# A hybrid decoder layer on one core: four edits in the order of ScalarE, in the head norms and in the branch stage

## The chip, the core and the metric

The kernel runs on one core of one Trainium2 chip. The metric is the device time of one execution in microseconds, the median of several. Engines: TensorE (PE, weight loads PEld), VectorE (DVE), ScalarE (ACT), GpSimd (POOL), SyncE (SP, which issues nearly all DMAs).

## The reference

One layer of a decoder on 1024 prompt tokens and 32 sample tokens (8 sequences of 4), model width 1024, all fp32. After an RMS norm one projection gives everything: queries, keys and values of branch A, the q/k/v channels and the gates of branch B, queries of branch C, and 3 x 1024 gate columns.

- Branch A: attention in a sliding window of 128 with a sink, 8 heads of 64 on 2 key heads.
- Branch B: a causal convolution of width 4 over 1536 channels, Silu, and the gated delta rule on 4 heads of 128. Its q and k are normalised per head and token: `x * rsqrt(sum(x * x) + eps)`. Eight such sums per token (4 heads of q, 4 of k) are the head squares.
- Branch C: attention to 256 memory rows, 4 heads of 128.

```python
up = jnp.einsum('blnc,ncd->blnd', branches, p['w_branch'])
gate = jax.nn.sigmoid(gates.reshape(Bsz, L, N_BRANCH, D_MODEL))
mix = jnp.sum(gate * up, axis=2) @ p['w_out']
x = x + _rms_norm(mix, p['ln_mix_post'])
h = _rms_norm(x, p['ln_ffn_pre'])
gt, uf = jnp.split(h @ p['w_ffn_in'], 2, axis=-1)
f = (jax.nn.silu(gt) * uf) @ p['w_ffn_out']
x = x + _rms_norm(f, p['ln_ffn_post'])
```

## The kernel before, in words

The 1056 token columns lie along the free axis in 3 chunks of 352. A weight panel is 128 output channels by 1024 inputs. Each fp32 product is made from three fp32r products: weights and activations are split into a high part (rounded) and a low part (what remains), and high x high, high x low and low x high are summed. GpSimd splits each panel in two passes (L853 high, L856 low; in the branch stage L922 and L924, in `split_to`) from `raw` into `wsp`, both with two slots: one panel is used while the next is split and the one after it is loaded. The semaphores `w_hi` and `w_lo` count these passes.

**First projection (to about 384 us).** 27 panels by `gemm` (L995, 72 matmuls). Panels 0 to 11 are branch B's channels: ScalarE evicts them into `cv`, VectorE runs the convolution, ScalarE the Silu into `y2`; for panels 0 to 7 ScalarE also writes the squares into `sqb`. `head_squares(n)` (L1000) runs on TensorE behind `gemm(n + 3)`: for each of the 9 token tiles the 128 tokens of `sqb` are the stationary operand and one column of ones the moving one, so that tile t's sum lands in a column of its own of bank 4, with the tokens along the partitions. That is how VectorE needs them in `ssq`, which ScalarE fills at L1733 behind the evictions of the narrow panel 12 (L1069, `b` and `a` of branch B). These gemms stand in a loop of four rounds of two panels.

**Tiles (385 to 863 us).** For each of 8 tiles of 128 tokens all engines follow one list, `TILE`. Each engine has its own reading of a step. "G" is a number of matmuls of the gate panels, laid between the others as cover. S(j) is a pair of score products of branch A (j below 4) or C: TensorE makes them, VectorE takes the row maximum (L2313, L2321), ScalarE exponentiates (L1846). T(j) transposes the result on TensorE, V(j) multiplies it with the values. Y(l) and X(l) are the two halves of level l of the inversion of branch B's triangular matrix: Y's product is copied to `yy` by ScalarE (L1833), and X (L1183, L1186) multiplies with `yy`. In ScalarE's reading the exponentials of S(j) belong to step S, so for j = 1 and j = 2 they stand ahead of the copies of Y(1) and Y(4).

**Samples (863 to 1014 us).** The same for the sample tokens, with eight more gate panels between. `gates(x)` evicts a gate chunk and stores it. ScalarE's last function other than a copy there is a square root (L1949).

**Branch stage (1014 to 1163 us).** 12 panels j of 256 output channels by 512 inputs (L1500), 4 per branch, each of two halves by three chunks in banks 0 to 2. ScalarE takes the Sigmoid of the two gate rows of the panel (L1967, loaded by `load_q`), VectorE multiplies the bank with them (L2548 for the first branch; L2553 into `prd` and L2555 into `accT` later) and so frees it. The three branches' activations come from memory into `brw` (`load_br`) and are split into `actD` by ScalarE and VectorE (L1957 and L2505 by chunk for the first, L1963 and L2523 later). Between the branch panels the eight parts of `w_out` are loaded and split: ScalarE makes the high part (L1979), GpSimd the low part (L943), in the order `W_SEQ`. SyncE issues in this order at the front: `load_wb(0)`, `load_br(0)`, `load_wb(1)`, gates 0 and 1, the store `o_z`, then it waits for `g_ad` and issues eight stores of the recurrent state (L750), the store `mem_o`, `load_br(1)`, and in the loop over j the next panel and the next gates.

Then follow the output projection (L1523), the norms and the FFN (L1508, L1569), which nothing of the change touches.

## Time and profile before

| | us |
|---|---|
| median of 3 executions | 2065.21 (2065.07 to 2067.7) |
| the profiled execution's own time | 2062.75 |
| its span in the profile | 2060.9 |

| engine | busy us | share |
|---|---|---|
| VectorE | 987.8 | 48% |
| ScalarE | 517.7 | 25% |
| GpSimd | 742.3 | 36% |

The mean granted clock is 0.997 of full speed. Most of TensorE's work is the fp32r matmul of 352 columns; a record of one lasts 323 ns, but they are pipelined and follow each other by about 160. In the rows below a line begins with start and length in us, and a bracket at its end is the idle time of the engine ahead of it and what ended that. PEld rows tell better than PE rows when TensorE could have gone on, since the ends of matmuls are modelled.

### The profile page before, as it was taken

What the parts mean: (1) busy time and instruction counts of PE and PEld (TensorE: products, weight loads), DVE (VectorE), ACT (ScalarE), POOL (GpSimd) and SP (SyncE); (2) the same over time, 40 slices, a digit from 0 to 9 for tenths busy, and PEclk for the clock granted to TensorE, in tenths of its full rate; (3) what the DMA queues carried; (4) which work ended last, traced back from release to release, by engine and by line L of the source; (5) the groups of instructions that cost most, each with busy time, mean ns of one, the idle gap of its engine ahead of it and who ended that gap; (6) DMA issues with size and microseconds to landing.
All of it is one profiled execution on the core that took longest, in us unless ns stands there. A gap on an engine that the chain in (4) does not pass through costs nothing.

```text
span 2060.9 us, 36132 instructions
## 1 busy us (share of the span) xinstructions
PE 2002.7 (97%) x14350; PEld 1903.8 (92%) x14350; DVE 987.8 (48%) x1761; ACT 517.7 (25%) x1151; POOL 742.3 (36%) x318
## 2 busy tenths in 40 slices
PE   6999999999999999999999999999999999999998
PEld 6999999888888889989799888999999999999997
DVE  6755630356565555322459745434353525253535
ACT  5333621243343444321232333100000000000002
POOL 3434774222111122123145322443434343434344
PEclk9999999999999999999999999999999999999999
DMA  5223333433233332263674421111111111111114
GB/s 189 92 83 100 109 114 99 146 105 88 61 99 88 100 91 68 78 190 120 204 247 159 150 104 67 42 51 41 51 41 51 41 51 41 51 41 51 41 41 179
DMA packets 221294, 193.91 MB, mean 94 GB/s; under 512 B 24731, under 2 KB 192283, under 8 KB 221170
## 3 DMA queue, kind: packets, MB, share of 16 engines
q1 hardware_dynamic: 207058, 182.72, 28.7%
q10 hardware_dynamic: 14128, 9.65, 1.6%
q8 instruction: 79, 1.29, 0.3%
q14 instruction: 29, 0.24, 0.0%
HBM read 146.26 MB, written 47.09 MB: 94 GB/s over the span
## 4 chain that ended last, share of the span: by engine, by line
PE 91%; DVE 3%; DMA 2%; ACT 1%; issue 1%; SPq 1%; POOL 0%; ACTq 0%; DVEq 0%; POOLq 0%
PE psum L1508 24%; PE psum L995 13%; PE psum L1569 11%; PE psum L1200 9%; PE psum L1523 5%; PE psum L1500 4%; PE psum L1278 4%; PE psum L1112 3%; PE psum L1247 2%; PE psum L1183 1%; PE psum L1236 1%; PE psum L1019 1%; PE psum L1060 1%; PE psum L1186 1%; ACT pr L1846 1%
## 5 line engine op out<-in xcount | busy, mean ns | idle before, releaser
L853 POOL TENSOR_TENSOR wsp<-raw,kc 128x1024 fp32r<-128x1024 f32 x115 | 279.5, 2430 | 1101.6 <-PE psum L1200 391.6
L1508 PE MATMUL psum<-actD,wsp 128*128 128x352 f32 x3168 | 515.8, 323 | 1.0 <-ACT sg L2052 0.6
L1508 PEld LDWEIGHTS psum<-actD,wsp 128*128 128x128 f32 x3168 | 509.0, 188 | 1.6 <-issue 0.9
L856 POOL TENSOR_TENSOR wsp<-raw,wsp 128x1024 fp32r<-128x1024 f32 x115 | 283.7, 2467 | 9.0
L995 PE MATMUL psum<-actT,wsp 128*128 128x352 f32 x1656 | 269.6, 323 | 0.0
L2640 DVE TENSOR_TENSOR accT<-accT,psum 128x352 f32<-128x352 f32 x504 | 241.7, 520 | 50.1 <-PE psum L1569 50.1
L995 PEld LDWEIGHTS psum<-actT,wsp 128*128 128x128 f32 x1656 | 264.8, 188 | 0.3
L1569 PE MATMUL psum<-fT,wsp 128*128 128x352 f32 x1512 | 249.8, 323 | 0.4 <-DVE accT L2640 0.4
L1569 PEld LDWEIGHTS psum<-fT,wsp 128*128 128x128 f32 x1512 | 244.0, 188 | 0.7 <-DVE accT L2640 0.7
L1200 PE MATMUL psum<-actT,wsp 128*128 128x352 f32 x1152 | 229.6, 338 | 0.0
L2623 DVE TENSOR_TENSOR fr<-psum,sg 128x352 f32<-128x352 f32 x66 | 34.5, 524 | 375.3 <-PE psum L1508 373.1
L1200 PEld LDWEIGHTS psum<-actT,wsp 128*128 128x128 f32 x1152 | 183.3, 189 | 4.1
L1500 PE MATMUL psum<-actD,wsp 128*128 128x352 f32 x864 | 142.1, 326 | 7.9 <-DVE prd L2553 3.8
L1500 PEld LDWEIGHTS psum<-actD,wsp 128*128 128x128 f32 x864 | 139.9, 190 | 10.1 <-DVE prd L2553 4.7
L2052 ACT ACTIVATE sg<-psum 128x352 f32<-128x352 f32 x66 | 30.5, 464 | 435.1 <-PE psum L1508 435.1
L1278 PE MATMUL psum<-actT,wsp 128*128 128x352 f32 x576 | 104.1, 331 | 0.0
L1278 PEld LDWEIGHTS psum<-actT,wsp 128*128 128x128 f32 x576 | 92.2, 190 | 5.5 <-issue 5.2
L2060 ACT ACTIVATE fT<-fr 128x352 fp32r<-128x352 f32 x66 | 32.8, 498 | 230.5 <-DVE fr L2623 230.5
L2137 DVE SCALAR_TENSOR_TENSOR y<-cv,scT,y 128x1024 f32<-128x1024 f32 x72 | 62.4, 913 | 0.9 <-DVE y L2137 0.4
L2134 DVE TENSOR_SCALAR y<-cv,scT 128x1024 f32<-128x1024 f32 (+1 forms) x24 | 29.8, 1283 | 59.1 <-ACT y L1700 55.4
L2222 DVE TENSOR_TENSOR kd<-psum,par 128x512 f32<-128x512 f32 x8 | 5.5, 692 | 105.5 <-PE psum L1121 105.5
L922 POOL TENSOR_TENSOR wsp<-raw,kc 128x1024 fp32r<-128x1024 f32 x13 | 25.8, 1981 | 77.7 <-DMA raw<-in_w_branch 40.6
(452 smaller groups left out, 2484.8 us busy)
## 6 DMA issues: line engine op xcount, KB each, us to landing
raw<-in_w_in SPq DMA_DIRECT2D x100, 256.0 KB, 4.0
raw<-in_w_ffn_in SPq DMA_DIRECT2D x88, 256.0 KB, 3.1
gat<-s_gate SPq DMA_DIRECT2D x12, 1056.0 KB, 5.0
raw<-in_w_ffn_out SPq DMA_DIRECT2D x44, 256.0 KB, 2.7
s_gate<-gst SPq DMA_DIRECT2D x48, 176.0 KB, 1.9
s_qkv<-y SPq DMA_DIRECT2D x12, 528.0 KB, 3.0
brw<-s_br SPq DMA_DIRECT2D x3, 2112.0 KB, 9.5
raw<-in_w_branch SPq DMA_DIRECT2D x24, 256.0 KB, 5.6
```

The lines of the kernel that those rows point to most:

```text
L853: pool.tensor_tensor(wsp[:, slot, 0], raw[:, slot], ones.unsqueeze(1).to_broadcast([P, KT, P]), ALU.mult).then_inc(w_hi, 1)
L856: pool.tensor_tensor(wsp[:, slot, 1], raw[:, slot], wsp[:, slot, 0].bitcast(F32), ALU.subtract).then_inc(w_lo, 1)
L995: mm = pe.matmul(psum[0:m, c, 0:CH], wsp[:, slot, a, k, 0:m], actT[:, h, k, CH * c:CH * c + CH], start=(k == 0 and q == 0), stop=(k == KT ...
L1112: mm = pe.matmul(psum[:, bank, w * h:w * h + w], lhs(h), rhs(h), start=True, stop=True)
L1200: mm = pe.matmul(psum[:, x % 2, 0:CH], wsp[:, (NPB + j) % 2, a, kt, :], actT[:, h, kt, CH * c:CH * c + CH], start=(n % 24 == 0), stop=(n % ...
L1278: mm = pe.matmul(psum[:, c, 0:CH], wsp[:, (NPB + m) % 2, a, k, :], actT[:, h, k, CH * c:CH * c + CH], start=(y % 24 == 0), stop=(y % 24 == ...
L1500: mm = pe.matmul(psum[:, c, 0:CH], slab(wsp[:, :, a], slot)[:, k, P * half:P * half + P], actD[:, h, a4 + k, CH * c:CH * c + CH], start=(k ...
L1508: mm = pe.matmul(psum[:, bank, 0:CH], wsp[:, slot, a, k, :], actD[:, h, k, CH * c:CH * c + CH], start=(k == 0 and q == 0), stop=(k == KT - ...
L1523: mm = pe.matmul(psum[0:rows, 3 + 2 * slot + half, :], actD[:, h, (k + 4) % 8, P * t:P * t + rows], wo_part(k, a)[:, 512 * half:512 * half ...
L1569: mm = pe.matmul(psum[:, 4 + x % 4, 0:CH], wsp[:, slot, a, m, :], fT[:, fs, h, CH * c:CH * c + CH], start=(q == 0), stop=(q == 2))
L2137: op = dve.scalar_tensor_tensor(out=dst[part], in0=src[part], scalar=w, in1=dst[part], op0=ALU.mult, op1=ALU.add)
L2640: dve.tensor_tensor(accT[:, m, cols], accT[:, m, cols], psum[:, 4 + x % 4, 0:CH], ALU.add).then_inc(o_ad, 1)
```

## The change

1. **Head squares.** The squares are now the moving operand and a 32-column stationary operand `row_n` is zero but for column n, which is one. The 1024 prompt tokens go as four groups of 256 columns into four groups of 32 partitions of bank 4, the 32 sample tokens into bank 3. All eight heads accumulate in the same place (`start` at n = 0, `stop` at n = 7). The loop of panels is unrolled, since n sets `start` and `stop`. The sums then have tokens along the free axis: ScalarE copies them to `mout`, TensorE transposes them with three instructions behind the narrow panel, and ScalarE copies into `ssq` after the Silu of panel 11. `one_col` lies in `tmp`, written by three small memsets at GpSimd's start.
2. **TILE.** A new step Z(j), read by ScalarE only, holds the exponentials of S(j). Z(1) stands behind Y(1) and Z(2) behind Y(4), each other Z directly behind its S.
3. **Front of the branch stage.** Branch panel 2 is loaded ahead of SyncE's wait for `g_ad`. ScalarE runs a Sigmoid of one column ahead of the eviction of the last three gate chunks. The Sigmoid of gate panel 0 runs in two halves, and VectorE waits for the first only before it multiplies the first three chunks.
4. **Quarter passes.** In `split_to` and the low part of a `w_out` panel, a pass over 1024 columns becomes four over 256, with one semaphore increment behind the last.

```diff
+    one_col = tmp[:].rearrange("p x t h -> p (x t h)")[:, 0:40]
-    TILE = (... ("S", 1), ("Y", 1), ("G", 4), ... ("S", 2), ("Y", 4), ("G", 4), ...)
+    TILE = (... ("S", 1), ("Y", 1), ("Z", 1), ("G", 4), ... ("S", 2), ("Y", 4), ("Z", 2), ("G", 4), ...)
@@ sync
         store_dec(1, "o_z")
+        load_seq(2, 3)
         sp.wait_ge(g_ad, 8)
...
             if j + 2 < 12:
-                load_seq(W_N["b", j + 1] - NPD + 1, W_N["b", j + 2] - NPD + 1)
+                if j > 0:
+                    load_seq(W_N["b", j + 1] - NPD + 1, W_N["b", j + 2] - NPD + 1)
@@ gpsimd
+        pool.memset(one_col[:, 0:7], 0.0)
+        pool.memset(one_col[:, 7:8], 1.0)
+        pool.memset(one_col[:, 8:40], 0.0)
...
-            pool.tensor_tensor(hi, src, ones[:, 0:1].to_broadcast([P, D]), ALU.mult).then_inc(w_hi, 1)
+            for k in range(0, D, 256):
+                op = pool.tensor_tensor(hi[:, k:k + 256], src[:, k:k + 256], ones[:, 0:1].to_broadcast([P, 256]), ALU.mult)
+            op.then_inc(w_hi, 1)
             pool.wait_ge(w_hi, n + 1)
-            pool.tensor_tensor(lo, src, hi.bitcast(F32), ALU.subtract).then_inc(w_lo, 1)
+            low_part(n, hi, lo)
+
+        def low_part(n, hi, lo):
+
+            src = raw[:, n % 2].rearrange("p k n -> p (k n)")
+            for k in range(0, D, 256):
+                op = pool.tensor_tensor(lo[:, k:k + 256], src[:, k:k + 256], hi[:, k:k + 256].bitcast(F32), ALU.subtract)
+            op.then_inc(w_lo, 1)
@@ tensor
             pe.wait_ge(sq_ok, n + 1)
-            for t in range(NT + 1):
-                r = P if t < NT else NS
-                mm = pe.matmul(psum[0:r, 4, bass.ds(n * (NT + 1) + t, 1)], sqb[:, P * t:P * t + r], ones[:, 0:1],
-                               start=True, stop=True)
+            row_n = one_col[:, 7 - n:39 - n]
+            for g in range(4):
+                pe.matmul(psum[32 * g:32 * g + 32, 4, 0:2 * P], row_n, sqb[:, 2 * P * g:2 * P * g + 2 * P],
+                          start=(n == 0), stop=(n == 7))
+            mm = pe.matmul(psum[0:32, 3, 0:NS], row_n, sqb[:, SEQ:SEQ + NS], start=(n == 0), stop=(n == 7))
             mm.then_inc(ss_mm, 1)
...
-        with pe.Fori(0, 4) as i:
-            for b in range(2):
-                gemm(2 * i + 3 + b, 1 - b)
-                head_squares(2 * i + b)
+        for n in range(8):
+            gemm(n + 3, 1 - n % 2)
+            head_squares(n)
...
+        pe.wait_ge(sq_ok, 8 + 1)
+        for u in range(2):
+            pe.transpose(psum[:, 4, P * u:P * u + P], mout[:, 0, P * u:P * u + P], ident)
+        pe.transpose(psum[0:NS, 3, 0:32], mout[0:32, 0, 2 * P:2 * P + NS], ident[0:32, 0:32]).then_inc(ss_mm, 1)
@@ scalar
         act.wait_ge(ss_mm, 9)
+        act.activation(mout[:, 0, 0:2 * P], psum[:, 4, 0:2 * P], ACT.Copy)
+        act.activation(mout[0:32, 0, 2 * P:2 * P + NS], psum[0:32, 3, 0:NS], ACT.Copy).then_inc(sq_ok, 1)
...
-        ssps = psum[:, 4, 0:8 * (NT + 1)].rearrange("p (n t) -> p n t", n=8)
-        act.activation(ssq[:, :, 0:NT], ssps[:, :, 0:NT], ACT.Copy)
-        act.activation(ssq[0:NS, :, NT:NT + 1], ssps[0:NS, :, NT:NT + 1], ACT.Copy).then_inc(ssq_ok, 1)
         silu(11, 1, 16 * 5 + 16)
+        act.wait_ge(ss_mm, 10)
+        for u in range(2):
+            act.activation(ssq[:, :, u:NT:2], psum[:, 4, P * u:P * u + P].rearrange("p (g n) -> p n g", n=32)[:, 0:8, :], ACT.Copy)
+        act.activation(ssq[0:NS, :, NT], psum[0:NS, 3, 0:8], ACT.Copy).then_inc(ssq_ok, 1)
...
+                elif step[0] == "Z":
+                    j = step[1]
                     act.wait_ge(a_nm, 6 * t + j + 1)
...
         gates(20)
+        act.activation(dsm[:, 18:19], dsm[:, 1:2], ACT.Sigmoid)
...
             act.wait_ge(q_in[j % 2], 16 * (j // 2) + 16)
+            if j == 0:
+                act.activation(gat[:, 0, 0], gat[:, 0, 0], ACT.Sigmoid).then_inc(q_sg, 1)
+                act.activation(gat[:, 0, 1], gat[:, 0, 1], ACT.Sigmoid).then_inc(q_sg, 1)
+                return
@@ vector
-            dve.wait_ge(q_sg, j + 1)
+            dve.wait_ge(q_sg, j + 2 if j > 0 else 1)
...
             for half in range(2):
+                if j == 0 and half == 1:
+                    dve.wait_ge(q_sg, 2)
```

## Rows read from the trace of the kernel before

**Rows 1.** The page, part 1: busy us (share of span), instructions, per engine.
```profile
PE 2002.7 (97%) x14350; PEld 1903.8 (92%) x14350; DVE 987.8 (48%) x1761; ACT 517.7 (25%) x1151; POOL 742.3 (36%) x318
```

**Rows 2.** Waits of TensorE: engine, line, releaser: us in total, times, longest.
```profile
PE psum L1183 <- ACT yy L1833: 20.9, 16, 1.6
...
PE psum L1500 <- DVE prd L2553: 3.8, 3, 1.8
```

**Rows 3.** The chain in order of time: start us, us, what. Panels 3 and 11.
```profile
67.51 11.53 PE psum L995 x72
...
175.74 11.72 PE psum L995 x72
```

**Rows 4.** Timeline 900 to 910, TensorE, last row its weight loads.
```profile
900.72 1.09 PE L1337 MATMUL psum<-kc,ck 128*128 128x128 f32 x8
901.57 2.96 PE L1278 MATMUL psum<-actT,wsp 128*128 128x352 f32 x17
904.46 0.64 PE L1344 MATMUL psum<-ckT,qw 128*32 128x256 f32 x8
...
905.03 0.85 PEld L1337 LDWEIGHTS psum<-kc,ck 128*128 128x128 f32 x8 [0.41 <-issue]
```

**Rows 5.** Timeline 165 to 212, ScalarE: Silu of panels 9 and 10.
```profile
187.99 2.08 ACT L1700 ACTIVATE y<-y 128x1056 f32<-128x1056 f32 x2
```

**Rows 6.** Timeline of tile 2, the steps S(1) to T(1) and Y(4) to T(2).
```profile
516.40 0.68 PE L1168 MATMUL psum<-xx,atl 64*64 64x64 f32 x16
...
517.33 0.16 DVE L2321 SCALAR_TENSOR_TENSOR asm<-asm,snk 128x2 f32<-128x2 f32 x1
517.52 0.51 ACT L1846 ACTIVATE pr<-pr,asm 128x256 f32<-128x256 f32 x1 [1.68 <-DVE asm L2321]
...
518.52 0.36 ACT L1833 ACTIVATE yy<-psum 128x256 f32<-128x256 f32 x1
...
518.94 0.27 PE L1183 MATMUL psum<-yy,xt 64*64 64x64 f32 x1 [1.02 <-ACT yy L1833]
...
521.30 0.66 PE L1236 MATMUL psum<-kc,pr 128*128 128x128 f32 x4
...
529.75 0.36 ACT L1833 ACTIVATE yy<-psum 128x256 f32<-128x256 f32 x1
...
532.54 0.66 PE L1236 MATMUL psum<-kc,pr 128*128 128x128 f32 x4
```

**Rows 7.** Timelines of the front of the branch stage, ScalarE and weight loads.
```profile
999.81 0.46 ACT L1893 ACTIVATE gst<-psum 128x352 f32<-128x352 f32 x1 [5.40 <-PE psum L1278]
...
1019.91 1.28 ACT L1967 ACT_TABLE_LOAD   x1
1021.20 3.82 ACT L1967 ACTIVATE gat<-gat 128x2112 f32<-128x2112 f32 x2
...
1023.83 18.85 PEld L1500 LDWEIGHTS psum<-actD,wsp 128*128 128x128 f32 x108 [2.53 <-DVEq L2550]
```

**Rows 8.** Windows: length, busy per engine, granted clock, DMA share, GB/s.
```profile
1024.00:1026.00 2.00, 2.00 (x9) 2.00 (x10) 0.92 (x2) 1.02 (x1) 1.07 (x1) 0.61 1.13 334
1026.00:1028.00 2.00, 2.00 (x9) 2.00 (x8) 0.53 (x1) 0.00 (x0) 0.00 (x0) 0.54 0.62 157
```

**Rows 9.** Timelines of panel 2: gate DMA's issue, its Sigmoid, TensorE's loads.
```profile
1032.02 0.36 SPq L685 DMA_DIRECT2D gat<-s_gate  x1
...
1041.37 1.97 ACT L1967 ACTIVATE gat<-gat 128x2112 f32<-128x2112 f32 x1 [16.34 <-DMA gat<-s_gate]
...
1043.12 2.06 PEld L1500 LDWEIGHTS psum<-actD,wsp 128*128 128x128 f32 x13 [0.43 <-POOL wsp L924]
```

**Rows 10.** Timeline of the middle of the branch stage, a GpSimd pass and VectorE.
```profile
1092.99 2.55 POOL L924 TENSOR_TENSOR wsp<-raw,wsp 128x1024 fp32r<-128x1024 f32 x1
1093.21 3.44 DVE L2523 TENSOR_TENSOR actD<-brw,actD 128x1056 fp32r<-128x1056 f32 x1
...
1097.14 11.81 PE L1500 MATMUL psum<-actD,wsp 128*128 128x352 f32 x72 [1.81 <-DVE prd L2553]
```

**Rows 11.** One line's instructions: durations in ns, min, median and max.
```profile
L881 POOL TENSOR_TENSOR wsp<-raw,wsp x1: 323/323/323, 174.5 to 174.5; 128x64 fp32r<-128x64 f32 x1
```

More of the change, by code:

```diff
@@ L277, in build @@
     gs_st = [sem(f"gs_st{c}") for c in range(3)]
-    TILE = ("KV", "DEC", ("S", 0), "KK", ("G", 12), ("T", 0), ("G", 8), ("V", 0), "INV", ("G", 8), ("E", 0), ("S", 1), ("Y", 1), ("G", 4),
[5 rows of a table removed]
+    TILE = ("KV", "DEC", ("S", 0), ("Z", 0), "KK", ("G", 12), ("T", 0), ("G", 8), ("V", 0), "INV", ("G", 8), ("E", 0), ("S", 1), ("Y", 1),
[6 rows of a table added]
     assert sum(step[1] for step in TILE if step[0] == "G") == 144
@@ L942, in _ @@
                     pool.sem_inc(w_hi, 1)
-                    pool.tensor_tensor(lo, raw[:, n % 2].rearrange("p k n -> p (k n)"), hi.bitcast(F32), ALU.subtract).then_inc(w_lo, 1)
+                    low_part(n, hi, lo)
         split_at(NPF, NPF % 2, 32 * (NPF // 2) + 32, 6 + UO - 6)
```

11 rows, old and new, of the table TILE are left out of this document.

## The prediction

> **What bounds the kernel now.** I read the busy line of the page first: TensorE is busy 97% of the span [rows 1]. A gain can only be matrix work taken away or one of TensorE's waits taken away, so the second view was the waits of TensorE alone [rows 2]: 20.9 us in 16 waits for the copy `yy` of ScalarE, and in the branch stage 3.8 us in 3 waits for VectorE's product `prd`. The third was the chain in order of time, where the first projection panels start at a fixed pitch [rows 3]. Last came timelines of the four places that the diff touches: one head-squares block, one tile, the front of the branch stage and its middle. The profiled execution took 2062.75 us (span 2060.9), 2.46 us below the median of the runs, 2065.21. I sum changes against the former and add the sum to the latter.
>
> **1. Head squares (8 blocks).** Eight panels with their blocks lie between 67.51 and 175.74, 13.53 us each, and a panel alone takes 11.53 [rows 3]. A block costs 2.00, and the panel behind the last one takes 11.72 instead of 11.53: 16.2 us in all. The new block is four fp32 products with 32 stationary and 256 moving columns, one in each column group, and one of 32 moving columns. The trace has exactly the four (L1344): eight records in 0.64 us, and in the round of 4.31 us in which they stand (900.15 to 904.46: the start 0.57 before the next line's 900.72) 17 projection matmuls of 0.16 and 0.85 of transposes leave 0.74 for them, with the idle of the weight loads before and behind them (0.41 behind) [rows 4]. The fifth adds 0.1 by my estimate (two short records; a transpose record there is 0.11 of pitch). So 8 x 0.84 = 6.7 replaces 16.2: **-9.5 us**. Bounds: if the four did not overlap, each would run two records of twice the 0.107 pitch of a 128-column record, 1.7 + 0.3 per block, and nothing is gained (0); if the fifth is free, -10.3. I take the row of the same shape. The loop of panels unrolled costs nothing: the unrolled panels show the same 11.5.
>
> The Trainium skill, "TensorEngine Tiling (Array Packing)", Key Properties, says that changing the tiling mode drains the engine, which speaks against this block since it adds two changes. The trace agrees with it (0.41 us without a weight load behind L1344) [rows 4], and the 0.74 already holds it.
>
> **2. The turn-back.** New on TensorE are three transposes (0.107 each) with a wait for ScalarE's copy of the sums. That copy stands behind the Silu of panels 9 and 10, which ends at 190.07, and takes some 0.5; TensorE is at its place at 195.1, after the 48 matmuls of the narrow panel [rows 5]. The wait is covered by 4.5 us; if it were not, the next panels would be held by what is missing. The later copy into `ssq` moves behind the Silu of panel 11, and the evictions of panel 13 start 0.4 us later, with 5 us left. **+0.4 us** (0.3 to 1.5).
>
> **3. The exponentials behind the copies (8 tiles).** In the ScalarE order only the pairs for heads 1 and 2 move. Before, in tile 2, the exponentials wait for VectorE's row maximum (517.33 + 0.16), run 517.52 to 518.5, and only then the copy of Y(1) runs at 518.52, though its matmuls ended at 516.40 + 0.68 = 517.08; TensorE stands until 518.94 for it. The same at 529.75 for Y(4) [rows 6]. 1.0 + 1.6 = 2.6 per tile, and each of the eight tiles has these two waits: 20.9 in all [rows 2]. With the copy first it ends at 517.5, before the four covering matmuls do (4 x 0.16 behind 517.08), and X(1) starts at once. The exponentials don't get later, because they wait for the maximum until 517.5 anyway. What is late next: the transposes T(1), which need them. They end at 518.6; T(1) stands at 521.30, 1.0 earlier then: 1.7 us of margin. For head 2 they end at 529.7, and T(2) stands at 532.54 - 1.6 = 530.9: 1.2 us. The next copy, Y(2), stands at 520.4. All the rest of a tile moves with TensorE, since VectorE's, GpSimd's and the loads' waits there are for TensorE. **-20.9 us**; bounds -21 and, if T gave back the exponentials' 1.1 us each time, -3.
>
> **4. The front of the branch stage.** Before: table load 1019.91 to 1021.19, two Sigmoids of 2112 wide in 3.82 us, and behind the first multiply TensorE's loads resume at 1023.83 after 2.53 us idle [rows 7]. The new Sigmoid of one column draws the table load to a place where ScalarE idles 5.40 us before 999.81 [rows 7]: free. The Sigmoid of half a panel starts at 1019.9, ends at 1020.9, the multiply takes 0.5, and TensorE resumes at about 1021.7 where its loads end at 1021.3. Of the 2.24 us for which TensorE stood, 0.3 remains: -1.9. After the idle the granted clock was 0.54 from 1026 to 1028 and about 0.6 in the two us before, which is its 1.2 GHz level in most of these 4 us [rows 8]: 2 x 0.46 + 2 x 0.39 = 1.7 us lost. I expect it to stay at the upper level without that idle: -1.7.
>
> The panel loaded early (panel 2) waits on SyncE for GpSimd's split of panel 0, done 2 us before the queued state stores may start (1010.3 against 1012.3 in the timeline), so these, `mem_o` and the second `brw` load are delayed by at most its own 1.4 us. It ends TensorE's wait of 0.43 at 1043.12 [rows 9]; without it the 3.6 us won above would be given back there, because GpSimd's split waited for this DMA. But the gates of panel 2 are issued at 1032.02 behind the `brw` load and arrive at 1041.37 [rows 9]. TensorE will be at panel 2 at 1039.0 and want its first bank back at 1044.8; Sigmoid, one high part, one low part and a multiply (2.0 + 1.0 + 1.3 + 0.5) behind an arrival at 1040.9, half a us sooner than now, end at 1045.7 to 1046. So I add +1.2 (0 to 3). Front: -1.9 - 1.7 - 0.4 + 1.2 = **-2.8 us** (-4.3 to +1).
>
> **5. Quarter passes.** A VectorE operation with both inputs in SBUF ends only after the GpSimd pass that is running: the 1056-wide subtraction took 3.44 us at 1093.21 against GpSimd's pass 1092.99 to 1095.54 (1.25 us alone: 1095.5 + 1.2 = 1096.7), and TensorE then waited 1.81 [rows 10]. The rule behind it: the Trainium skill, "SBUF — State Buffer", Who interferes with whom, says such a pair is held for a whole instruction and the other blocks; the trace agrees. With passes of 256 columns the block is at most one quarter. A quarter's price is not in the trace: between 0.32 (64 columns, L881) [rows 11] and a whole 2.55; on the line through 64 and 1024 columns 0.32 + 192/960 x 2.2 = 0.77, and 0.6 for the first kind. I take 0.7. The eight of a panel then need 5.6 us instead of 4.4, inside 11.5 us of TensorE per panel; the panel-1 split ends at 1026.3, 1.2 us before its use. Of the 3.8 us of waits [rows 2] I expect 0.8 to stay: **-3.0 us** (-3.8 to +6).
>
> **Sum.** -9.5 + 0.4 - 20.9 - 2.8 - 3.0 = -35.8. 2062.75 becomes 2026.9; on the median 2065.2 becomes **2029.4 us**.
>
> **Rivals.**
> (a) The tile wait moves: T(1) and T(2) wait for the exponentials, or Y(2)'s copy does. For it: ScalarE waits for VectorE's maximum in each of these steps already. Against it: margins of 1.7 and 1.2. Half the gain gone: 2040.
> (b) Successive quarters follow so closely that VectorE isn't let in between. Then the 3 us of part 5 don't come: 2032.5. For it: no row has two GpSimd passes without a semaphore between them. Against: at each change of pass VectorE got in.
> (c) Column groups don't overlap in this block: +9.5, 2039. Against it stands L1344.
> (d) GpSimd becomes the bound of the branch stage. It has 132 quarters (12 panels of 8, seven `w_out` parts of 4, the last of 8) and is held during VectorE's two-input operations. In a panel with both kinds of work 12 x 0.7 + some 4 us of these is 12.4 against 11.5: slips of 1 us that the next panel makes good. At 1.0 a quarter six panels slip about 4: with part 5's 3 us and some of it made good, about 2047.
> (e) The slower side, by the same mechanism: a quarter costs about as much as a whole pass, 1.9, because the cost is per instruction. 132 x 1.9 = 251 us for a stage that takes 149 (1014.4 to 1163.3): +102 on the sum of parts 1 to 3 alone, 2065.2 - 30.0 + 102 = 2137. It decides from (149 + 30) / 132 = 1.36 us a quarter. The 0.32 us of the 64-column pass speaks against it.
>
> [...]
>
> **Chances.** Forecast 0.66; (a) 0.08; (b) 0.12; (c) 0.05; (d) 0.06; (e) 0.03. The range of the forecast itself is 2025 to 2034; with (a) to (c) and the other ends of part 4 it is **2021 to 2041**. No change can be told from 0.2%, about 4 us. Faster 0.95, same 0.02, slower 0.03.
>
> **What would show it.** Head squares: panels at a pitch of 12.4, five products in about 0.7 us. Tile: pitch 57.0 instead of 59.6, no wait of X for `yy` over 0.3 us, and T without a new wait on ScalarE. Front: no table load behind 1001, TensorE idle under 0.5 us before the fourth chunk, clock 1.00 throughout, and a wait of about 1 us in panel 2 whose chain leads to the gate DMA. Quarters: passes of 0.5 to 0.8 us, VectorE's accumulation never over 1.3. The forecast is wrong if panels keep 13.5, if T waits for `pr`, or if TensorE waits for GpSimd's `wsp` in the branch stage.

## The result, and the profile after

The changed kernel takes 2031.41 us (median of 4 runs, 2028.47 to 2033.52), the kernel before 2065.64 (4 runs): ratio 0.9832, 95% interval 0.9814 to 0.9849. Forecast were 2029.4 us and a range of 2021 to 2041. Nine runs of the changed kernel, with those of the experiments, have their median at 2030.5. The profiled execution took 2032.34 us (span 2030.5), 30.4 less than that of before, which had been 2.5 to 3 us below its own median.

The 95% interval of a ratio is about 0.0014 to each side, some 3 us, and the experiments ran on three chips, on which the kernel before has medians of 2065.3 to 2066.9. Two kernels whose medians differ by less than about 4 us are therefore told apart by the waits in their profiles and not by their times. In experiment 8 one of six executions took 3257.58 us at a granted clock of 0.557, and is left out of the times.

Busy time of the page, and the waits of TensorE (us in total, times, longest), as [rows 1, 2] of before:

```profile
PE 1992.1 (98%) x14289; PEld 1891.0 (93%) x14289; DVE 973.4 (48%) x1761; ACT 519.8 (26%) x1156; POOL 772.9 (38%) x420
```

```profile
PE psum L1313 <- DMA da<-s_qc: 4.1, 1, 4.1
PE psum L1520 <- DVE actD L2535: 3.1, 3, 2.5
PE psum L1520 <- DVEq L2582: 2.2, 1, 2.2
PE psum L1520 <- POOL wsp L939: 1.4, 2, 1.1
```

The waits for `yy` (20.9 us) and `prd` (3.8) are gone. The first two that remain existed before:

```profile
PE psum L1293 <- DMA da<-s_qc: 2.3, 1, 2.3
PE psum L1500 <- DVE actD L2505: 1.7, 3, 1.1
```

Both grew: the wait for the transfers of `da` from 2.3 to 4.1 us, the one before the branch stage from 1.1 to 2.5. Neither belongs to a line that the change touches.

Positions of TensorE's work give the ledger (differences of the two profiled executions, each step taken from the start of one stage to the start of the next):

| stretch | before | after | difference | forecast |
|---|---|---|---|---|
| start to first such panel | 67.51 | 67.98 | +0.5 | 0 |
| eight panels with head squares | 13.53 each | 12.32 each | -9.7 | -9.5 |
| narrow panel, turn-back, to the tiles | | | +0.6 (turn-back 0.35) | +0.4 |
| eight tiles | 476.1 | 452.7 | -23.3 | -20.9 |
| first gate products of the sample stage, to the da transfers | 15.0 | 16.8 | +1.8 | 0 |
| from there to the branch stage | 136.5 | 140.7 | +4.2 | 0 |
| branch stage | 148.8 | 144.4 | -4.4 | -5.8 |
| rest | 897.6 | 897.6 | 0 | 0 |

The sum is -30.4; forecast was -35.8. By the medians the gain is 34.2. The branch stage of the changed kernel took 144.4 us here and 146.1 in the second profile of the same kernel (experiment 1), so a difference of 1 to 2 us in that stage is not by itself the effect of an edit.

**Panels.** Timeline of TensorE in the changed kernel: start us, us, line, shapes, count. They answer [rows 3].

```profile
80.06 11.81 PE L1011 MATMUL psum<-actT,wsp 128*128 128x352 f32 x72
91.79 0.64 PE L1021 MATMUL psum<-sqb,tmp 128*32 128x256 f32 x8
...
92.40 11.81 PE L1011 MATMUL psum<-actT,wsp 128*128 128x352 f32 x72
```

The pitch is 12.34, so a block costs 0.81 on the 11.53 of a panel alone, where the forecast had 0.84. The four products start at 91.79 and the next panel at 92.40.

**One tile.** Timeline, the steps that [rows 6] show of before:

```profile
501.58 0.38 ACT L1856 ACTIVATE yy<-psum 128x256 f32<-128x256 f32 x1 [1.29 <-PE psum L1188]
501.77 0.16 DVE L2351 SCALAR_TENSOR_TENSOR asm<-asm,snk 128x2 f32<-128x2 f32 x1
501.97 0.51 ACT L1871 ACTIVATE pr<-pr,asm 128x256 f32<-128x256 f32 x1
502.29 0.27 PE L1203 MATMUL psum<-yy,xt 64*64 64x64 f32 x1
504.67 0.66 PE L1256 MATMUL psum<-kc,pr 128*128 128x128 f32 x4
```

The copy now runs first, the exponential starts 0.04 us behind VectorE's maximum as before, X(1) has no idle in its row, and the transposes T(1) (L1256) have none either.

**Front of the branch stage.** ScalarE, then the weight loads (answers to [rows 7]), then a window of 4 us with the granted clock behind the busy times (answers to [rows 8]):

```profile
967.46 1.28 ACT L1976 ACT_TABLE_LOAD   x1 [0.39 <-ACT gst L1918]
987.34 1.66 ACT L1983 ACTIVATE actD<-brw 128x352 fp32r<-128x352 f32 x4 [14.40 <-DMA brw<-s_br]
993.83 1.07 ACT L1994 ACTIVATE gat<-gat 128x1056 f32<-128x1056 f32 x1
1016.08 1.97 ACT L1997 ACTIVATE gat<-gat 128x2112 f32<-128x2112 f32 x1 [17.32 <-DMA gat<-s_gate]
```

```profile
988.50 1.92 PEld L1520 LDWEIGHTS psum<-actD,wsp 128*128 128x128 f32 x12 [2.73 <-issue]
995.61 23.05 PEld L1520 LDWEIGHTS psum<-actD,wsp 128*128 128x128 f32 x144 [0.29 <-DVEq L2582]
1021.16 40.39 PEld L1520 LDWEIGHTS psum<-actD,wsp 128*128 128x128 f32 x252 [2.49 <-DVEq L2582]
1062.89 11.55 PEld L1520 LDWEIGHTS psum<-actD,wsp 128*128 128x128 f32 x72 [1.35 <-POOL wsp L939]
```

```profile
992.00:996.00 4.00, 3.70 (x22) 3.15 (x21) 3.06 (x8) 3.61 (x6) 1.24 (x3) 1.00 1.06 283
```

The table load stands 21 us ahead of the stage. The idle before the fourth chunk, 2.53 us in the weight loads before, is 0.29, and the clock stays at 1.00, its upper level of 2.4 GHz. At 1021.16 TensorE waits for panel 2's multiply: its Sigmoid could start only at 1016.08, when the gates had landed, 10.4 us behind their issue. The row at 1062.89 is new: TensorE waits for GpSimd.

**Quarters.** One line's instructions: minimum, median, maximum in ns, first and last start. They answer [rows 10, 11].

```profile
L930 POOL TENSOR_TENSOR wsp<-raw,kc x52: 605/614/1628, 977.8 to 1135.6; 128x256 fp32r<-128x256 f32 x52
L939 POOL TENSOR_TENSOR wsp<-raw,wsp x52: 724/742/1752, 980.2 to 1139.6; 128x256 fp32r<-128x256 f32 x52
L2587 DVE TENSOR_TENSOR accT<-accT,prd x48: 524/576/1093, 1041.4 to 1136.5; 128x352 f32<-128x352 f32 x48
```

VectorE's accumulation took up to 2.62 us before and takes at most 1.09 now.

### The profile page after: what moved, and what is told of

It reads as the page before. It is cut to its first block, busy times and chain, and to the rows that moved or that the text cites. A ratio compares the mean times of both kernels' runs of the same rounds, so it can differ in the third digit from the quotient of the medians.

```text
span 2030.5 us, 36004 instructions
## 1 busy us (share of the span) xinstructions
PE 1992.1 (98%) x14289; PEld 1891.0 (93%) x14289; DVE 973.4 (48%) x1761; ACT 519.8 (26%) x1156; POOL 772.9 (38%) x420
## 4 chain that ended last, share of the span: by engine, by line
PE 92%; DMA 3%; DVE 2%; SPq 1%; POOL 1%; issue 1%; ACT 0%; ACTq 0%; DVEq 0%; POOLq 0%
PE psum L1528 25%; PE psum L1011 13%; PE psum L1589 11%; PE psum L1220 10%; PE psum L1543 5%; PE psum L1520 4%; PE psum L1298 4%; PE psum L1132 3%; PE psum L1267 2%; PE psum L1188 1%; PE psum L1203 1%; PE psum L1256 1%; PE psum L1076 1%; PE psum L1241 1%; PE psum L1036 1%; PE psum L1206 1%
## 5 line engine op out<-in xcount | busy, mean ns | idle before, releaser
L860 POOL TENSOR_TENSOR wsp<-raw,kc 128x1024 fp32r<-128x1024 f32 x115 | 279.7, 2432 | 1067.8 <-PE psum L1220 368.2
L1520 PE MATMUL psum<-actD,wsp 128*128 128x352 f32 x864 | 140.3, 323 | 6.6 <-DVE actD L2535 3.1
L930 POOL TENSOR_TENSOR wsp<-raw,kc 128x256 fp32r<-128x256 f32 x52 | 38.1, 763 | 62.0 <-DMA raw<-in_w_branch 37.5
```

The source lines that it names most:

```text
L860: pool.tensor_tensor(wsp[:, slot, 0], raw[:, slot], ones.unsqueeze(1).to_broadcast([P, KT, P]), ALU.mult).then_inc(w_hi, 1)
L1520: mm = pe.matmul(psum[:, c, 0:CH], slab(wsp[:, :, a], slot)[:, k, P * half:P * half + P], actD[:, h, a4 + k, CH * c:CH * c + CH], start=(k ...
```

## Experiments

Unless told otherwise an experiment is an edit of the changed kernel. "Before" in a ratio is the kernel before, run on the same chip.

**1. The changed kernel again.** No edit.

> The changed kernel itself, unaltered, for a second profile and as the yardstick of its neighbours on the same chip. Between the profiled executions so far the same load of brw took 9.5, 8.9, 11.8, 12.1, 11.1 and 8.7 us from issue to use, and the wait for da was 2.3 or 2.4 in the two kernels with the old head squares and 4.0 to 4.4 in those with the new. Theory A: the brw time is a draw of each execution; a second profile of the same program may show anything from 8.7 to 12, and its span goes with it (2027 to 2032). Theory B: it is fixed by the program: 11.8 again, and 2.5 us of idle before the branch stage again. Both expect 4.1 us for da.

2029.65 us (2028.08 to 2033.15, 5 runs), ratio 0.9819 (0.9806 to 0.9833). The profiled execution waited 3.4 us for `da`, and `brw` took 11.81 us, against 11.78 in the first profile. So two executions of this program agree in the `brw` time, as theory B says, and differ by 0.7 us in the wait for `da`, which both theories had at 4.1.

**2. The tile order alone**, on the kernel before.

```diff
-    TILE = (... ("S", 1), ("Y", 1), ("G", 4), ...
+    TILE = (... ("S", 1), ("Y", 1), ("Z", 1), ("G", 4), ...
```

> The kernel before with one part of the change alone: in the ScalarE order of a tile the exponentials of heads 1 and 2 stand behind the copies of Y. Theory A (the ledger of the two traces): tile pitch 56.8 instead of 59.6, the end of the eight tiles 23.3 us earlier, no wait of X for yy; the wait for the transfer of da behind the tiles, 2.3 us before and 4.1 after the whole change, does not hang on this part and is a matter of when the transfers happen to land: 2.3 to 4 us here; the whole kernel -21 to -23.5, 2042 to 2044. Rival B: the denser tiles are what makes that wait longer, so it is 4 us or more here and 1.3 us of slower clock come with it: -20, 2045. Rival C: 2.0 us per tile only comes in company with the other edits; pitch 57.0 and -20.9 as predicted at the end of the tiles.

2042.64 us, ratio 0.9887 (0.9872 to 0.9903): -22.7 us, theory A. The tiles take 452.7 us here too, and the wait for `da` is 2.4 us. The forecast of 2.6 per tile misses two things. A tile has shrunk by 2.77: each resumption of TensorE behind a wait had cost 0.08 more than the row's idle. And the stage had lost clock behind its waits: in the profile of before the first tile took 60.9 us, not 59.6. Windows of the kernel before, then of this one (busy PE, PEld, DVE, ACT, POOL, then granted clock):

```profile
406.91:416.91 10.00, 8.41 (x114) 6.90 (x110) 3.67 (x12) 2.83 (x9) 0.00 (x0) 0.83 0.00 0
```

```profile
408.10:418.10 10.00, 10.00 (x138) 8.63 (x138) 4.53 (x11) 3.29 (x9) 0.00 (x0) 1.00 0.14 43
```

8 x 2.77 + 1.3 = 23.5, and 23.3 is measured. How often the clock falls differs between profiles with the old order: in experiment 4 the eight tiles took 479.1 us, with a mean clock of 0.97 in four of them, in experiment 3 476.4, with 0.97 in one. In all eleven profiles with the new order they took 452.6 to 452.8. So part of the gain depends on how often the old order lost clock in the execution that it is compared with.

**3. The head squares alone**, with turn-back and written-out panels, on the kernel before.

```diff
-        with pe.Fori(0, 4) as i:
...
+        for n in range(8):
+            gemm(n + 3, 1 - n % 2)
+            head_squares(n)
...
```

> The kernel before with one part of the change alone: head squares in four column groups, the turn-back and the panels written out instead of looped. Theory A: panels at 12.35 instead of 13.55, the turn-back +0.35, the start of the tiles 8.6 us earlier, the tiles at 59.6 each; and the wait for da behind the tiles is 2.3 us as before, since no transfer there was touched: 2056.5 to 2057. Rival B: with this part the wait for da is 4 us or more (it was 2.4 with the tile part alone, 4.0 to 4.4 in every kernel with the head squares), and the lower clock behind it comes too: 2059 to 2060.

2061.98 us (12 runs, 2054.05 to 2066.33), ratio 0.9975 (0.9963 to 0.9987). Neither number was right; rival B came nearest. The panels and the turn-back gain what they should: the sample stage starts 9.2 us earlier. Then 2.2 are lost up to the `da` transfers (wait 4.5), 3.2 between them and the branch stage (`brw` took 11.0 us instead of 9.5), and 1.9 in the branch stage, where TensorE waits 2.7 us for the split of panel 2, which [rows 9] show as 0.43. Of 9.2 us 1.9 are left in this profiled execution, 5 by the medians. So about half of this part is given back when it stands alone; the profile of before makes it look like more, for it had a short wait in panel 2 that the other kernels with the old front did not have:

```profile
PE psum L1499 <- POOL wsp L924: 3.0, 1, 3.0
```

This is experiment 4, in which no work differs from the kernel before; with the tile order alone the wait is 3.0 us too. The early load of panel 2 thus removes about 3 us in three of four such profiles, where the forecast read 0.4.

**4. The panels written out, nothing else**, on the kernel before (the diff of experiment 3 with the old head squares).

> The kernel before with one edit that changes no work: TensorE's eight panels with head squares are written out instead of looped. In all kernels with the new head squares (which had to be written out) the stretch from the first gate matmul behind the tiles to the first product of the branch stage took 155 to 158 us, in the two kernels without them 150.5 and 151.5, though no edit touches it (apart from the late brw load, its parts are the wait for da and the clock behind it). Theory A: what matters is the program as it lies in memory, longer by the written-out panels: the stretch takes 155 or more here too, the panels keep 13.5 us, and the kernel is 3 to 5 us slower than before, 2069. Rival B: it is something that the head squares themselves do: the stretch keeps 151 us, 2065.

2065.55 us, ratio 0.9990 (0.9980 to 1.0001): no change. The stretch has 151.7 us, `da` 2.0, `brw` 9.3. Theory A (the program's place in memory) is out.

**5. Four more products per block**, into a bank that nobody reads.

```diff
             row_n = one_col[:, 7 - n:39 - n]
+            for g in range(4):
+                at = 0 if n < 4 else 32 * g
+                pe.matmul(psum[at:at + 32, 6, 0:2 * P], row_n, sqb[:, 2 * P * g:2 * P * g + 2 * P], start=True, stop=True)
```

> The changed kernel with products added that nobody reads: ahead of each head-squares block four more products of the same shape into a free bank, in panels 3 to 6 all four in one column group, in panels 7 to 10 one in each of the four groups. Theory A (the forecast's price and its rival c): the four in four groups overlap and add 0.5 to 0.75 us to the pitch of 12.35, the four in one group don't and add 1.7 us. Rival B: what is saved is not the overlap but the eight weight loads of the old block; then both kinds add the same, 0.7 us or less. Rival C: both add 1.7, and the new block's price is low for another reason.

One run, 2033.69 us. TensorE's timeline, a panel of each kind; L1022 is the added four products, and the block itself stands behind them:

```profile
82.33 11.81 PE L1011 MATMUL psum<-actT,wsp 128*128 128x352 f32 x72
94.06 1.70 PE L1022 MATMUL psum<-sqb,tmp 128*32 128x256 f32 x7
...
96.40 11.81 PE L1011 MATMUL psum<-actT,wsp 128*128 128x352 f32 x72
...
137.36 11.79 PE L1011 MATMUL psum<-actT,wsp 128*128 128x352 f32 x72
149.09 0.64 PE L1022 MATMUL psum<-sqb,tmp 128*32 128x256 f32 x8
...
150.13 11.79 PE L1011 MATMUL psum<-actT,wsp 128*128 128x352 f32 x72
```

Pitch 96.40 - 82.33 = 14.07 with one group, +1.72 on 12.35; with four groups 150.13 - 137.36 = 12.77, +0.42. So the overlap is real and worth 1.3 us a block. That is theory A, and rivals B and C are out, with the overlapped four cheaper than I had said: 0.42, where they stand right ahead of products of their own shape. And this kernel has the new head squares and yet waits 1.7 us for `da`, with `brw` at 9.5: so the head squares don't lengthen the transfers by themselves either, as rival B of experiment 4 would have it. TensorE reaches the branch stage without idle here and then waits 3.6 us in panel 2 for the gates, where the changed kernel waits 2.2: what was won ahead of that transfer is given back at it.

**6. More gate products ahead of the wait for `da`.**

```diff
-        gate_mm(78)
+        gate_mm(94)
...
-            gate_mm(17)
+            gate_mm(17 if b else 11)
```

> The changed kernel with 16 of the sample stage's gate matmuls (0.16 us each, 2.6 us) moved ahead of TensorE's wait for the transfers of da (6 taken from the first cache round, 10 from the end). Theory A: the wait of 4.1 us is for a transfer with a fixed landing time; it falls to 1.5 and the stretch at the lower clock behind it gets shorter: -2.6 to -4 us, 2027.5 to 2029. Rival B: the wait falls but a later wait of TensorE takes its place, in the first cache round or before the branch stage, where the moved matmuls were cover: 0 to -1, 2031. Rival C: the clock falls behind the wait all the same, 1.3 us of the loss stay: -2.6.

2030.66 us, ratio 0.9833 (0.9820 to 0.9847): nothing gained. The wait for `da` fell to 1.4, the one for `del_` rose from 0.6 to 3.8 us. This is rival B, but not for lack of cover. The timeline of this kernel beside it:

```profile
861.65 2.40 POOL L860 TENSOR_TENSOR wsp<-raw,kc 128x1024 fp32r<-128x1024 f32 x1 [6.23 <-PE psum L1298]
862.12 2.08 DVE L2421 TENSOR_TENSOR ddc<-ddc,dmr 32x128 f32<-32x128 f32 x1
864.94 1.67 DVE L2428 TENSOR_TENSOR dxt<-dat,kc 32x128 f32<-32x128 f32 x1
```

In the changed kernel L2421 takes 0.27. The gate products that now end earlier let GpSimd split the next panel earlier, right beside VectorE's chain of small operations with both inputs in SBUF. L2421 ends at 864.20, 0.15 us behind GpSimd's first pass, and L2428 at 866.61, 0.14 behind its second. It is the same mechanism as in part 5 of the prediction, found in another stage: what the earlier work triggered cost what it had won.

**7. Panel 2 loaded in its old place.**

```diff
-        load_seq(2, 3)
         sp.wait_ge(g_ad, 8)
...
-                if j > 0:
-                    load_seq(...)
+                load_seq(...)
```

> The changed kernel with one part undone: the raw values of branch panel 2 are loaded in their old place, behind the state stores and the second brw load. Theory A: the early load shares the DMA engines with the first brw load, which took 11.8 us from issue to landing instead of 9.5; without it brw lands in 9.5 to 10 us, TensorE's idle before the branch stage falls from 2.5 to some 0.5 to 1, and panel 2 waits instead for GpSimd's split, 3 to 4 us where 2.2 was lost to the gates: net 0 to +1, 2031 to 2032.5. Rival B: brw is late for another reason, the idle stays at 2.5, and only the wait in panel 2 grows: +1 to +2. Rival C: the wait in panel 2 is set by the gates whatever the split does, and the brw gain is net: -1.5 to -2, 2029.5.

2034.87 us, ratio 0.9848 (0.9834 to 0.9861): +4.4 on the changed kernel's 2030.5; the branch stage takes 150.1 us, against 144.4 and 146.1. `brw` takes 11.1 us without the early load, so the early load isn't what makes it late (it was issued 7.5 us behind `brw`; in experiment 6 `brw` took 8.7 with it). TensorE waits in panel 2 for GpSimd:

```profile
1012.21 2.32 POOL L928 TENSOR_TENSOR wsp<-raw,kc 128x256 fp32r<-128x256 f32 x4 [13.41 <-DMA raw<-in_w_branch]
1014.61 2.77 POOL L937 TENSOR_TENSOR wsp<-raw,wsp 128x256 fp32r<-128x256 f32 x4
1017.44 0.95 PE L1518 MATMUL psum<-actD,wsp 128*128 128x352 f32 x2 [5.44 <-POOL wsp L937]
```

5.4 us against 2.2 for the gates: rival B's mechanism at about twice its price. The two passes take 5.1 us in quarters where they took 4.3 whole, so quarters explain at most 0.8 of it.

**8. The first Sigmoid whole, its table loaded late.**

```diff
-        act.activation(dsm[:, 18:19], dsm[:, 1:2], ACT.Sigmoid)
...
-            if j == 0:
-                act.activation(gat[:, 0, 0], gat[:, 0, 0], ACT.Sigmoid).then_inc(q_sg, 1)
-                act.activation(gat[:, 0, 1], gat[:, 0, 1], ACT.Sigmoid).then_inc(q_sg, 1)
-                return
...
```

> The changed kernel with one part undone: the Sigmoid of the first branch panel whole again, and its table loaded where it is first needed. Theory A (the forecast's step): TensorE idles 2.2 us instead of 0.3 before the fourth chunk, the granted clock falls to 0.5 or 0.6 for some 4 us behind it, 1.7 us lost: 3.6 us later at the end of panel 0. Of these the wait in panel 2 (2.2 to 2.4 us, for the gates) takes back what it can, since the gates' load is not bound to TensorE but to the state stores: net +1.4 to +1.6, 2031 to 2032.5. Rival B: the gates' load moves as well, the wait in panel 2 stays at 2.2 and all 3.6 us are seen: 2034. Rival C: no clock loss without the idle before it: net 0, 2029.6.

2030.77 us, ratio 0.9831 (0.9815 to 0.9847), the same as the changed kernel within what can be told. The idle before the fourth chunk is back (2.25 us), and so is the lower clock (0.62 from 992 to 996, where it was 1.00). The wait in panel 2 is gone instead: TensorE gets there later, and the gates are there. So the front is worth some 2.1 us of idle and 1.7 of clock, as forecast, and the gate transfer takes back 2.2 of these 3.8 us. The branch stage takes 145.5 us, between the 144.4 and 146.1 of the changed kernel's two profiles, where theory A expects 1.4 to 1.6 more. Rival C is out, since the clock does fall behind the idle; whether the last 1.5 us are won can't be told. I had put the back-payment at 1.2.

**9. The gates of panel 2 ahead of the second `brw` load.**

```diff
-        sp.wait_ge(f_st, F_ST)
-        load_br(1)
         for c in range(3):
             sp.wait_ge(gs_st[c], 16 + 16 * 24)
+        load_q(2)
+        sp.wait_ge(f_st, F_ST)
+        load_br(1)
...
-                load_q(j + 2)
+                if j > 0:
+                    load_q(j + 2)
```

> The changed kernel with one reordering on SyncE: the gates of branch panel 2 are loaded ahead of the wait for the state stores and of the second brw load, instead of behind both. Theory A: the wait of 2.2 us for the multiply behind that transfer (forecast as +1.2) is caused by the 2.1 MB brw load issued just before it; the gates now land 2 to 4 us earlier and the wait goes: -2.2 us, 2029. Rival B: the transfer is held up by the 2 MB of state stores, not by brw: it lands at the same time, 0. Rival C: brw comes later instead and the low parts for the second branch make TensorE wait in panel 3 or 4: 0 to +2.

2027.51 us, ratio 0.9807 (0.9793 to 0.9821): 3 us below the changed kernel's nine runs and 2.1 below its five runs on the same chip. By the times alone the two can't be told apart; the profile decides. The gates are issued at 1000.92, and their Sigmoid starts 5.4 us later, not 10.4:

```profile
1000.92 0.43 SPq L687 DMA_DIRECT2D gat<-s_gate  x1
1003.62 0.36 SPq L682 DMA_DIRECT2D brw<-s_br  x1
```

```profile
1006.35 1.97 ACT L1999 ACTIVATE gat<-gat 128x2112 f32<-128x2112 f32 x1 [9.22 <-DMA gat<-s_gate]
```

No wait in panel 2 is left, and the branch stage takes 142.2 us. This is theory A: the gates' 1.1 MB had stood behind the 2.1 MB of `brw`.

**10. Whole passes.** The splits of the branch panels and of `w_out` as one instruction each.

```diff
-            for k in range(0, D, 256):
-                op = pool.tensor_tensor(hi[:, k:k + 256], ...
+            pool.tensor_tensor(hi, src, ...
```

> The changed kernel with one part undone: GpSimd's splits of the branch panels and of w_out run as whole passes again. Theory A: the waits of TensorE for VectorE's prd come back (3.8 us in 3 waits before), the two waits for GpSimd's wsp (1.4 us) go: net +2.4 us against the changed kernel, 2034, VectorE's accumulation up to 2.6 us again. Rival B: GpSimd was what bounded the stage with quarters, and whole passes (4.3 instead of 5.2 us per panel) are no worse: 0 to -1.4, 2030 to 2031.5. Rival C: with a stage that starts denser the waits for prd grow: +4 or more, 2035.5.

2035.07 us, ratio 0.9846 (0.9831 to 0.9861): +4.6 on the changed kernel; the branch stage takes 147.7 us, 1.7 and 3.4 more than in the changed kernel's two profiles. The waits for `prd` are back (3.3 us in 4), those for GpSimd gone, and the one in panel 2 is 2.9 instead of 2.2: 2.6 us by the waits, as theory A has it. VectorE's accumulation takes up to 2.72 us again. Quarters do what they are for.

**11. Halves, with the gates as in 9.**

> The changed kernel with two edits: the reordering of the gates of panel 2 as in the run beside it, and GpSimd's passes of the branch stage as halves of 512 columns instead of quarters. Theory A: what costs is the passes' number: a half takes 1.1 us, a panel's split 4.5 instead of 5.2 us, so that the two waits for GpSimd (1.4 us) go, while a blocked VectorE operation waits at most for 1.1 us and the waits for prd stay under 1 us in all: with the gates' 2.2 us -3 to -3.6, 2028. Rival B: halves block VectorE enough to bring 1.5 to 2 us of the waits for prd back: -2 to -2.5, no better than quarters. Rival C: the waits for GpSimd have to do with VectorE holding the port and stay as they are: -2.2.

2024.34 us, ratio 0.9800 (0.9786 to 0.9815): 3.2 below experiment 9 on the same chip, which the times alone do not show. In its profile TensorE has no wait for GpSimd, for `prd` or for the gates:

```profile
L932 POOL TENSOR_TENSOR wsp<-raw,kc x26: 1035/1042/2057, 973.0 to 1124.7; 128x512 fp32r<-128x512 f32 x26
L941 POOL TENSOR_TENSOR wsp<-raw,wsp x26: 1272/1378/2325, 975.1 to 1127.5; 128x512 fp32r<-128x512 f32 x26
L2589 DVE TENSOR_TENSOR accT<-accT,prd x48: 524/817/1632, 1033.4 to 1128.4; 128x352 f32<-128x352 f32 x48
```

VectorE's accumulation is slower than with quarters (up to 1.63 us), but 1.63 fits into the chunk of 1.93 us that covers it. This is theory A. The stage itself is 1.9 us shorter (142.2 to 140.3), about the 1.7 us of experiment 9's two waits for GpSimd, and the idle before it 1.0 us (`brw` took 10.9 us), which no edit here explains.

**12. All of it together.** 9 and 11, the cover of 6 with GpSimd's colliding split in quarters, and the first `brw` load in three column chunks.

```diff
+        for c in range(2):
+            sp.dma_start(brw[:, :, CH * c:CH * c + CH], first[:, :, CH * c:CH * c + CH]).then_inc((k_in, p_in)[c], 16)
         sp.wait_ge(f_st, ...)
-        load_br(0)
+        sp.dma_start(brw[:, :, 2 * CH:], first[:, :, 2 * CH:]).then_inc(b_in, 16)
...
-            split_at(NPB + m, ..., 6 + UC + 3 * m - 3)
+            split_at(NPB + m, ..., 6 + UC + 3 * m - 3, 2 if m == 19 else KT)
```

> The changed kernel with five edits: the gates of branch panel 2 ahead of the second brw load; halves instead of quarters (both as run before, 2024.3); the 16 gate matmuls ahead of the wait for da, now with the one GpSimd split that collided there (VectorE's 32x128 subtraction took 2.08 us instead of 0.27 beside it) cut into quarters; and the first brw load in three column chunks, two of them ahead of the wait for the sample's store, each waited for by itself. Theory A: the wait for da falls from 3.4 to 0.8 without a new wait for del_ over 1.3 us, and less is lost to the clock: -2.5 to -3.5; the first chunk of brw lands in 5 us instead of 11, so TensorE's idle of 1.4 to 2.5 us before the branch stage goes: -1.4 to -2.2. 2018.5 to 2020.5. Rival B: quarters of 0.6 us still hold the chain of small VectorE operations up, and the wait for del_ comes to 2 us or more: 2021 to 2022. Rival C: the state stores and gate loads share the queue, the three-part load is no earlier: 2021.

2020.90 us (2019.53 to 2024.78), ratio 0.9788 (0.9771 to 0.9805): the fastest, 9.6 us below the changed kernel, though 0.4 above theory A. The wait for `da` is 0.8 us, that for `del_` 1.6: quarters hold VectorE up by 0.4 where a whole pass did by 1.8.

```profile
862.88 0.70 DVE L2439 TENSOR_TENSOR dxt<-kc,dxt 32x128 f32<-32x128 f32 x1
864.23 1.09 PE L1366 MATMUL psum<-kc,ck 128*128 128x128 f32 x8 [1.62 <-DVE del_ L2442]
975.38 1.66 ACT L1992 ACTIVATE actD<-brw 128x352 fp32r<-128x352 f32 x4 [9.56 <-DMA brw<-s_br]
979.52 0.69 DVE L2532 TENSOR_TENSOR sd<-sd,psum 128x512 f32<-128x512 f32 x1 [2.54 <-PE psum L1397]
980.78 3.46 PE L1529 MATMUL psum<-actD,wsp 128*128 128x352 f32 x20 [1.05 <-DVE actD L2544]
```

The first chunk of `brw` is used at 975.38, 6.8 us behind its issue. The idle before the branch stage is still 1.05 us, but now its cause is the order on VectorE: the low parts stand behind the last state addition (979.52), which waits for TensorE itself.

**What stays open: the length of the transfers behind the tiles.** From the issue of the last store of `oba` to the end of SyncE's wait, and from the issue of the first `brw` load to its use, the profiled executions had:

| kernel | store issued at | store, us | wait for da, us | brw, us |
|---|---|---|---|---|
| before | 863.95 | 4.0 | 2.3 | 9.5 |
| tile order alone | 841.76 | 4.1 | 2.4 | 8.9 |
| panels written out | 867.78 | 3.3 | 2.0 | 9.3 |
| four more products | 841.20 | 3.3 | 1.7 | 9.5 |
| head squares alone | 854.73 | 5.5 | 4.5 | 11.0 |
| the changed kernel, two profiles | 831.98, 832.79 | 5.0, 4.6 | 4.1, 3.4 | 11.8, 11.8 |
| whole passes | 831.27 | 5.3 | 4.4 | 12.1 |
| panel 2 in its old place | 832.43 | 5.0 | 4.0 | 11.1 |
| gates first | 832.01 | 4.6 | 3.5 | 11.7 |
| more cover | 831.62 | 5.0 | 1.4 (with 2.6 more cover) | 8.7 |
| halves | 830.88 | 4.6 | 3.4 | 10.9 |
| first Sigmoid whole | 831.08 | 4.7 | 3.8 | 11.1 |
| all together | 831.08 | 4.6 | 0.8 (with 2.6 more cover) | in three parts |

The store and the wait for `da` fall into two classes, and no edit separates them: the head squares are on both sides, the written-out panels too, the tile order too. What the two classes differ in is the time at which the stage comes, 841 and 864 to 868 against 831 to 833 and 855. That is a pattern in 14 profiles, not a cause. The `brw` times don't follow it: more cover has 8.7 us at 831.62.

Seven profiles (the changed kernel's two, whole passes, panel 2 in its old place, gates first, halves, first Sigmoid whole) have the same order of work up to these transfers, but for a table load in the last. They show 4.6 to 5.3 us for the store, 3.4 to 4.4 for the wait and 10.9 to 12.1 for `brw`. What is known of `brw` is that it shares: the DMA engines' mean busy share is 1.00 from 1003.8 to 1013.8 before (297 GB/s) and 1.03 from 975.6 to 987.4 after (320 GB/s), with a branch panel and two loads of gates issued within 3.5 us behind it. Why the same transfers take 1 to 2 us longer in one program than in another, the runs don't say.

## Why the prediction was right, and where it was off

The total was forecast within 2.0 us and in its range, and most steps of the profile came as named, but part of that nearness is luck. In the profiled pair the tiles gained 2.4 us more than forecast, and the other stretches together some 8 less, for a gain 5.4 us smaller than forecast. The medians show 1.6 less, because the execution profiled of before was 2.9 us below the median of its kernel and that of after 0.9 above. The wait for the split of panel 2 is of that size, 0.43 us in that execution and 2.7 to 3.0 in three others with the old front, but that it is the difference isn't shown.

1. **Head squares:** right. -9.7 against -9.5. The overlap taken from L1344 holds (experiment 5), so rival (c) is out: in one group the four would have cost 1.3 us more in each block. The turn-back is right (+0.35 of +0.4).
2. **Tiles:** the mechanism right, the term too small: -23.3 against -20.9. The tile shrank by 2.77 us where its two rows of idle give 2.61, which is 0.08 more at each of the 16 resumptions (1.3 us), and the lower clock in the first tile (1.3 us) was not looked for. No wait went to T, so rival (a) is out.
3. **Front:** the step "Front: -1.9 - 1.7 - 0.4 + 1.2" was wrong in its last term. The idle, the clock and the table load came as said, but the gate transfer took back 2.2 to 2.4 us at its wait (experiment 8), so that this part is worth about -1.8 us in the profiled pair and not -2.8. Two things were missed. The early load was to delay the state stores by at most its own 1.4 us; its two issues took 5.66 us on SyncE, and the stores began at 988.76, where without it (experiment 7) they began at 984.21:

```profile
983.05 5.66 SPq L664 DMA_DIRECT2D raw<-in_w_branch  x2
```

And the gates came 10.4 us behind their issue, where 9.35 had been read from [rows 9]. They were issued 0.5 us behind `brw`, where before it had been 3.5 (the load of panel 2 had stood between), and they shared the DMA engines with it. The order of the two issues was the thing to look at (experiment 9).
4. **Quarters:** right in kind. 0.61 and 0.74 us for an undisturbed quarter, 0.76 and 0.88 in the mean, against 0.7. VectorE is let in between them, for its accumulation never takes over 1.09 us, while four quarters last 2.4 and more, so rival (b) is out. The waits for `prd` went from 3.8 to nothing. But a panel's eight take 6.6 us with VectorE beside them, not 5.6, and GpSimd was late twice: 1.4 us, where I had 0.8 left over. Rival (d) is there in a small size; it is what halves remove. Rival (e) is out by the price. The prediction's own sign of failure, "if TensorE waits for GpSimd's `wsp`", came true with 1.4 us and cost little. 

   The Trainium skill, "SBUF — State Buffer", Who interferes with whom, says that a VectorE instruction with two SBUF inputs contends with a GpSimd instruction that reads SBUF, and that the port pair they share is an exclusive lock. The trace agrees: in experiment 6 a subtraction of 0.27 us took 2.08 beside a whole pass.
5. **What the sum did not hold:** +1.8 up to the `da` transfers and +4.2 behind them. Of these 6 us, 1.8 are the wait for `da`, some 1.3 the clock behind it (0.52 over 6 us, where before two windows of 2 us at 0.50 and 0.73 were followed by 1.00), 1.4 the idle before the branch stage, and 1.6 a second stretch of lower clock. Windows of the kernel before, then of the changed one, the clock behind the five busy times:

```profile
878.00:880.00 2.00, 1.98 (x8) 1.85 (x9) 1.81 (x7) 0.00 (x0) 0.00 (x0) 0.50 1.07 362
880.00:882.00 2.00, 2.00 (x13) 1.83 (x12) 0.72 (x2) 0.00 (x0) 0.47 (x1) 0.73 1.09 357
```

```profile
848.00:850.00 2.00, 2.00 (x9) 1.87 (x10) 1.81 (x7) 0.00 (x0) 0.00 (x0) 0.50 1.07 305
852.00:854.00 2.00, 2.00 (x10) 1.95 (x10) 0.00 (x0) 0.00 (x0) 1.92 (x2) 0.60 0.67 165
889.80:929.80 40.00, 39.56 (x311) 35.80 (x310) 8.27 (x27) 8.17 (x26) 9.19 (x4) 0.96 0.54 169
```

I had treated the stage between tiles and branches as moving with TensorE. It has two waits for transfers in it, and those took longer; why they did is open.

## What to carry to other kernels

An early gain is paid out only as far as the next wait that is not bound to the engine that gained: list the transfers behind each shortened stage, with their issue order, before adding the gain to the sum. When work is brought forward, ask what its end releases on the other engines; here a GpSimd split came to lie beside VectorE's chain, and a new wait of 3.2 us took back the 2.7 that had been won. And cut a blocking pass only so fine that the blocked operation still fits into its cover: with halves of 1.0 to 1.4 us the waits for GpSimd that quarters had brought were gone, since each cut adds to the engine that is cut. A last one: before a term is read from one profile, ask whether another execution shows the same number; the wait for the split of panel 2 was 0.43 us in the one read and about 3 in three others.

## What the hardware showed that I had not expected

- Idles of 1.0 and 1.6 us in the first tile were followed by a clock of 0.83 over 10 us (1.3 us lost), while the same waits in a later tile left it at 1.00, and in experiment 4 four of the eight tiles had a mean of 0.97; the idle of 2.2 us in panel 2 of the changed kernel left it at 1.00, and that of 2.25 us at the fourth chunk in experiment 8 did not (0.62).
- Four fp32 products of 256 columns cost 0.42 us together in four column groups, and 0.43 us each in a single one.
- The same store took 3.3 to 4.1 or 4.6 to 5.5 us, and the same load 8.7 to 12.1 us, in different programs. Two executions of one program gave 5.0 and 4.6, and 11.78 and 11.81.
- Two DMA issues on SyncE took 5.66 us in all, where the pair ahead of them took 1.26, and held up the stores behind them.
